# Experts in pairs, and half of the output columns combined on TensorE

## The reference

```python
scores = sigmoid(x2d @ router)               # (272, 64)
# keep 4 of 8 groups of experts, then the 8 best experts of each token
gate = take_along_axis(scores, idx); gate = gate / sum(gate) * 2.5
def expert_block(tok, e, gt):                # tok: the tokens that chose expert e
    y = (silu(x2d[tok] @ w_gate[e]) * (x2d[tok] @ w_up[e])) @ w_down[e]
    return y * gt[:, None]
routed = segment_sum(y, slot_tok)            # the 8 expert outputs of each token, added
f = swiglu(x2d, sh_gate, sh_up, sh_down) + routed
h = layer_norm(ALPHA * h + f, ln_ffn_g, ln_ffn_b)
```

## Time and profile before

| | |
|---|---|
| time, median of 3 runs | 1658.77 us (1658.12 to 1667.34) |
| span of the profiled execution | 1659.9 us |
| TensorE / weight loads / VectorE / ScalarE / GpSimd busy | 89% / 57% / 37% / 19% / 20% |
| mean granted TensorE clock | 0.968 |
| moved by DMA | 508.21 MB, mean 306 GB/s |
| expert loop, layer 0 / layer 1 | 388.5 to 902 us / 1102.5 to 1617 us |

### The profile page before, as it was taken

How to read it: one execution, slowest core, us unless ns; L and a number is a source line. 1 busy time by engine, 2 the same in 40 slices (tenths; PEclk the granted TensorE clock), 3 DMA queues, 4 the chain that set the end, 5 groups by cost and what they waited for, 6 DMA issues and landing times.

```text
span 1659.9 us, 33659 instructions
## 1 busy us (share of the span) xinstructions
PE 1469.7 (89%) x12824; PEld 952.7 (57%) x12824; DVE 619.0 (37%) x1580; ACT 318.7 (19%) x743; POOL 331.5 (20%) x412
## 2 busy tenths in 40 slices
PE   6989988899998888888888698999998888888886
PEld 4776877656665555555554267466655555555542
DVE  5362352673333333333332704543333333333327
ACT  1521332110111111111111015111111111111110
POOL 6012000021222222222221210122222222222210
PEclk9999988899999999999999799999999999999998
DMA  6330002349999999999997961299999999999986
GB/s 198 124 113 1 4 4 80 105 175 370 403 414 415 416 415 415 415 416 415 415 416 312 366 184 52 94 376 396 414 415 416 416 415 415 416 415 416 416 339 246
DMA packets 139862, 508.21 MB, mean 306 GB/s; under 512 B 29273, under 2 KB 58273, under 8 KB 104188
## 3 DMA queue, kind: packets, MB, share of 16 engines
q1 hardware_dynamic: 103312, 456.49, 68.9%
q0 software_dynamic: 22288, 41.89, 7.0%
q10 hardware_dynamic: 14172, 8.54, 1.8%
HBM read 501.38 MB, written 36.90 MB: 324 GB/s over the span
## 4 chain that ended last, share of the span: by engine, by line
PE 44%; SPq 23%; DMA 22%; DVE 6%; issue 3%; ACT 1%; ACTq 0%; DVEq 0%; POOL 0%; POOLq 0%
SPq L844 23%; DMA arena<-in_moe_w_up 21%; PE ps L781 9%; PE ps L1423 6%; PE ps L799 3%; PE ps L1553 3%; PE ps L1006 2%; PE ps L1865 2%; PE ps L1967 2%; PE ps L762 1%; PE ps L769 1%; PE ps L1748 1%; DMA arena<-routed 1%; PE ps L1849 1%; PE ps L998 1%
## 5 line engine op out<-in xcount | busy, mean ns | idle before, releaser
L781 PE MATMUL ps<-arena 128*64 128x256 f32 x2048 | 234.5, 381 | 57.2 <-DMA arena<-in_moe_w_up 57.2
L781 PE MATMUL ps<-ring,arena 128*64 128x256 f32 x2048 | 234.6, 381 | 51.8 <-DMA ring<-in_moe_w_up 38.5
L774 DVE COPY arena<-ps 128x512 f32<-128x512 f32 x128 | 88.6, 692 | 514.1 <-PE ps L769 514.1
L781 PEld LDWEIGHTS ps<-arena 128*64 128x64 f32 x2048 | 163.4, 137 | 151.5 <-issue 106.4
L818 POOL DMA_INDIRECT arena<-hrows,arena x128 | 129.7, 1013 | 586.0 <-DVE arena L814 572.0
L781 PEld LDWEIGHTS ps<-ring,arena 128*64 128x64 f32 x2048 | 154.5, 137 | 154.0 <-issue 79.0
L823 POOL DMA_INDIRECT routed<-arena x128 | 118.2, 924 | 240.2 <-DVE arena L942 175.8
L942 DVE TENSOR_SCALAR arena<-ps,arena 64x512 f32<-64x512 f32 x128 | 95.1, 743 | 162.1 <-PE ps L799 162.1
L896 ACT COPY arena<-ps 128x256 f32<-128x256 f32 x128 | 47.6, 372 | 537.0 <-PE ps L781 537.0
L906 ACT ACTIVATE arena<-ps,arena 64x512 f32<-64x512 f32 x128 | 87.5, 683 | 206.1 <-PE ps L799 206.1
L799 PE MATMUL ps<-ring,arena 128*64 128x512 f32 x512 | 124.0, 605 | 0.0
(11 more groups left out here) (375 smaller groups left out, 1595.4 us busy)
## 6 DMA issues: line engine op xcount, KB each, us to landing
ring<-in_moe_w_gate SPq DMA_DIRECT2D x64, 1024.0 KB
ring<-in_moe_w_up SPq DMA_DIRECT2D x64, 1024.0 KB
ring<-in_moe_w_down SPq DMA_DIRECT2D x64, 1024.0 KB
arena<-in_moe_w_gate SPq DMA_DIRECT2D x64, 1024.0 KB
arena<-in_moe_w_up SPq DMA_DIRECT2D x64, 1024.0 KB
arena<-in_moe_w_down SPq DMA_DIRECT2D x64, 1024.0 KB
arena<-routed SPq DMA_DIRECT2D x16, 1024.0 KB, 14.3
ring<-in_attn_w_qkv SPq DMA_DIRECT2D x6, 1024.0 KB
```

The source lines that it names most:

```text
L774: return nc.vector.tensor_copy(xgT.rearrange("p (r j) m -> p j r m", r=2), ps[:, bU, :].rearrange("p (j r m) -> p j r m", j=4, r=2))
L781: mm = nc.tensor.matmul(dst[SLOTS * j:SLOTS * j + SLOTS, 0:FF], xgT[:, k, :], slot_of(s + j)[:, FF * k:FF * k + FF], start=(k == 0), stop= ...
```

## The change

Experts are handled in pairs (the code says "duo"). A pair shares one set of marks, one pick (three matmuls with six columns of values in place of three), one gather of 128 whole rows and one scatter of 128 rows of 512 columns. The gathered rows are turned in two halves, in the turns of the two experts ahead, into one of two `xgT` buffers. Output columns 0 to 511 ("far") are scaled by the gate and scattered as before. Columns 512 to 1023 ("near") are only copied by ScalarE; VectorE builds a matrix `spread_T` of 128 slots by 272 tokens that holds the gates, and TensorE multiplies the two into the PSUM banks 1 and 7 (and bank 0 for the last 16 tokens), where all pairs add up over the loop. These matmuls (`pe_combine`) stand in the odd expert's turn, for the pair before. The second half of the shared expert is done whole in the turns of experts 0 and 1. After the loop, the shared expert's `down` is split likewise: three tiles with columns 0 to 511, and `mm_combine` for the rest (`sda`). The rows that are loaded back and added are 512 wide.

```diff
-HEAD = 5
-TAIL = 3
+HEAD = 4
+TAIL = 4
+DUOS = E // 2
+COLS = D // 2
...
-        routed = [nc.dram_tensor(f"routed{l}", (T * TOPK, D), F32, kind="Internal").ap() for l in range(2)]
-        hrows_d = [nc.dram_tensor(f"hrows{l}", (2 * T, D // 2), F32, kind="Internal").ap() for l in range(2)]
+        routed = [nc.dram_tensor(f"routed{l}", (T * TOPK, COLS), F32, kind="Internal").ap() for l in range(2)]
+        hrows_d = [nc.dram_tensor(f"hrows{l}", (T, D), F32, kind="Internal").ap() for l in range(2)]
...
-        bV, bU, bG, bR, bY = 0, 2, 3, 4, (5, 6)
+        bU, bG, bR, bY = 2, 3, 4, (5, 6)
+        bA = (1, 7)
+        few_acc = ps[:, 0, 0:P]
+        picked = ps[:, bG, FF:FF + 6]
...
+        def mm_turn_x(dst, rows, half):
             for j in range(4):
-                mm = nc.tensor.transpose(dst[:, P * j:P * j + P], rows[:, P * j:P * j + P], ident[:, :])
+                mm = nc.tensor.transpose(dst[:, P * j:P * j + P], rows[:, P * (4 * half + j):P * (4 * half + j) + P],
+                                         ident[:, :])
             return mm
-        def copy_xt():
-            return nc.vector.tensor_copy(xgT.rearrange("p (r j) m -> p j r m", r=2),
-                                         ps[:, bU, :].rearrange("p (j r m) -> p j r m", j=4, r=2))
+        def copy_xt(dst, half):
+            return nc.vector.tensor_copy(dst[:, 4 * half:4 * half + 4, :],
+                                         ps[:, bU, :].rearrange("p (c m) -> p c m", c=4))
...
+        def mm_combine(of_slots, rows, start, stop):
+            for t in range(NT - 1):
+                nc.tensor.matmul(ps[:, bA[t], :], of_slots[:, P * t:P * t + P], rows, start=start, stop=stop)
+            for q in range(4):
+                mm = nc.tensor.matmul(few_acc[32 * q:32 * q + META, :], of_slots[:, 2 * P:T], rows[:, P * q:P * q + P],
+                                      start=start, stop=stop, tile_position=(0, 32 * q))
+            return mm
...
+        def mark_slots(pos, first_slot):
+            for par in range(2):
+                cols = slice(SLOTS * par, SLOTS * par + SLOTS)
+                last = nc.vector.scalar_tensor_tensor(
+                    out=hot[:, :, cols], in0=iota_s[:, cols].unsqueeze(1).to_broadcast([P, NT, SLOTS]),
+                    scalar=float(first_slot + 1), in1=pos[:, :, par:par + 1].to_broadcast([P, NT, SLOTS]),
+                    op0=ALU.add, op1=ALU.is_equal)
+            return last
...
+        def take_index(at, gate_of):
+            for par in range(2):
+                rows = slice(SLOTS * par, SLOTS * par + SLOTS)
+                nc.vector.tensor_scalar(at[rows, :], picked[rows, 3 * par:3 * par + 2], OUT_OF_RANGE, None, ALU.add)
+                last = nc.vector.tensor_copy(gate_of[rows, :], picked[rows, 3 * par + 1:3 * par + 3])
+            return last
...
+        def spread_gates(gate_of):
+            return nc.vector.tensor_scalar(spread_T, iota_t, gate_of[:, 0:1], gate_of[:, 1:2], ALU.is_equal, ALU.mult)
...
+        def pe_pick(pe, L, a):
+            pe.wait_ge(L.onehot, duo_num(a, L.duo_base + 1))
+            wait(pe, L.index, duo_num(a, L.duo_base))
+            mm_pick(picked, values_of_duo(a)).then_inc(L.values, 1)
+        def pe_turn_x(pe, L, a, half):
+            b = a[1] // 2 % 2
+            if half == 0:
+                pe.wait_ge(L.gathered[b], duo_num(a, 8 * L.duo_base + 16, 16, 2))
+            wait(pe, L.xt_copied, num(a, 1, L.base + half))
+            mm_turn_x(ps[:, bU, :], xs[b], half).then_inc(L.xt, 1)
+        def pe_combine(pe, L, l, a):
+            pe.wait_ge(L.spread, duo_num(a, L.duo_base + 1))
+            pe.wait_ge(L.near, num(a, 1, L.base + 2))
+            if early(a, 0):
+                pe.wait_ge(*moe_dve[l].at("sm1"))
+            mm_combine(spread_T, near[a[1] // 2 % 2], early(a, 0), False).then_inc(L.combined, 1)
...
-            after, three_after, prev = ahead(e, 1), ahead(e, 3), e_before(e)
+            prev = e_before(e)
             if this:
                 s0, s1, _ = e_slots(e)
-                pe.wait_ge(L.xt_copied, num(e, 1, L.base + 1))
+                pe.wait_ge(L.xt_copied, num(first_of(e), 1, L.base + 2))
                 pe.wait_ge(slot_loaded[s0], num(e, 16, L.slot_base[s0] + 16, per=SETS))
                 pe.wait_ge(slot_loaded[s1], num(e, 16, L.slot_base[s1] + 16, per=SETS))
-                wait(pe, L.gu_copied, num(e, 1, L.base))
-                mm_gate_up(ps[:, bG, :], s0).then_inc(L.gu, 1)
-            if this and after:
-                pe_turn_x(pe, L, l, plus(e, 1))
-            if this and three_after:
-                pe_pick(pe, L, plus(e, 3))
-            if this:
+                if early(e, 0):
+                    pe.wait_ge(L.index, L.duo_base + 2)
+                else:
+                    wait(pe, L.gu_copied, num(e, 1, L.base))
+                if e[1] % 2 and exists(first_of(e, 2)):
+                    pe.wait_ge(L.index, duo_num(first_of(e, 2), L.duo_base + 1))
+                mm_gate_up(ps[:, bG, :], s0, xgT[e[1] // 2 % 2][:, :, side(e)]).then_inc(L.gu, 1)
+                if exists(first_of(e, 1)):
+                    pe_turn_x(pe, L, first_of(e, 1), e[1] % 2)
+                if e[1] % 2 and e_before(first_of(e)):
+                    pe_combine(pe, L, l, first_of(e, -1))
                 copied, hidden = num(e, 1, L.base + 1), num(e, 1, L.base)
                 if not isinstance(copied, int):
                     pe.reg_add(copied_count, copied_count, 1)
...
                     copied, hidden = copied_count, hidden_count
                 pe.wait_ge(*moe_dve[l].at("choice"))
                 pe.wait_ge(L.gu_copied, copied)
+                if e[1] % 2 == 0 and exists(first_of(e, 2)):
+                    pe_pick(pe, L, first_of(e, 2))
                 wait(pe, L.hid, hidden)
                 mm_turn(ps[:, bR, :]).then_inc(L.turned, 1)
...
-                act.wait_ge(L.index, num(q, 1, L.base + 1))
-                wait(act, L.scattered[q[1] % 4], num(q, 16, 4 * L.base, per=4))
-                nc.scalar.activation(ysc[q[1] % 4][:, 512:1024], ps[SLOTS:P, bY[q[1] % 2], :], ACT.Copy,
-                                     scale=gate_s[q[1] % 8][SLOTS:P]).then_inc(L.y_a, 1)
+                wait(act, L.combined, duo_num(first_of(q), L.duo_base - 1))
+                nc.scalar.copy(near[q[1] // 2 % 2][side(q), :], ps[other_side(q), bY[q[1] % 2], :]).then_inc(L.near, 1)
...
-                wait(dve, L.scattered[q[1] % 4], num(q, 16, 4 * L.base, per=4))
-                nc.vector.tensor_scalar(ysc[q[1] % 4][:, 0:512], ps[0:SLOTS, bY[q[1] % 2], :],
-                                        gate_s[q[1] % 8][0:SLOTS], None, ALU.mult).then_inc(L.y_v, 1)
+                dve.wait_ge(L.index, duo_num(first_of(q), L.duo_base + 1))
+                nc.vector.tensor_scalar(far[b][side(q), :], ps[side(q), bY[q[1] % 2], :], gate_s[b][side(q), 1:2], None,
+                                        ALU.mult).then_inc(L.far, 1)
...
             def turn(e):
-                if ahead(e, 3):
-                    pool_gather(pool, L, l, plus(e, 3))
+                if e[1] % 2:
+                    return
+                if exists(plus(e, 4)):
+                    pool_gather(pool, L, l, plus(e, 4))
                 if e_before(e):
-                    pool_scatter(pool, L, l, plus(e, -1))
+                    pool_scatter(pool, L, l, plus(e, -2))
             over_experts(pool, turn)
-            pool_scatter(pool, L, l, (0, E - 1))
+            pool_scatter(pool, L, l, (0, E - 2))
...
-                if early(e, 2):
+                    mm_shared(pe, l, "sg1", range(KC))
+                if early(e, 1):
                     pe.wait_ge(*moe_dve[l].at("sm0"))
-                if isinstance(e[0], int) and e[1] < 4:
-                    mm_shared(pe, l, ("sg1", "su1")[e[1] // 2], range(KC // 2 * (e[1] % 2), KC // 2 * (e[1] % 2) + KC // 2))
+                    mm_shared(pe, l, "su1", range(KC))
...
-                for u in range(6):
-                    r0, n = TILES[u // 2]
+                pe.wait_ge(main.index, main.duo_base + DUOS)
+                for u, (r0, n) in enumerate(TILES):
                     for j in range(2):
-                        m = mm_(ps[0:n, SD_BANKS[u], :], shm[:, j, r0:r0 + n],
-                                shared_w[2][:, D * j + 512 * (u % 2):][:, 0:512], start=(j == 0), stop=(j == 1))
+                        m = mm_(ps[0:n, SD_BANKS[u], :], shm[:, j, r0:r0 + n], shared_w[2][:, D * j:D * j + COLS],
+                                start=(j == 0), stop=(j == 1))
                     m.then_inc(*st.step("sd", u))
+                pe_combine(pe, main, l, (0, E - 2))
                 pe_spill(pe, l)
+                for j in range(2):
+                    m = mm_combine(shm[:, j, :], shared_w[2][:, D * j + COLS:D * j + D], False, j == 1)
+                m.then_inc(*st.step("sda"))
...
                     for k in ON_PE:
                         pe.wait_ge(routed_loaded[t][k // 2], 16 * (l + 1))
```

(19 more changed lines are left out.)

375 lines of the change are left out of this document (189 added, 186 removed).

## The result

The changed kernel takes 1679.61 us (median of 4 runs, 1672.39 to 1690.51) where the kernel before takes 1660.3 in the same rounds: a ratio of 1.011, 95% interval 1.007 to 1.015, so it is slower by some 1%. The forecast was 1640. The profiled execution is the fastest of the four: 1672.39 us with a span of 1670.7, against a span of 1659.9 before. So it shows 10.8 us of a loss whose median is 19.

The account below looks back on a forecast made before the run. The weight stream (DMA) was taken to bound the loop late on, TensorE close behind. Per layer -10.5 + 2.0 + 2.7 = -5.8 us, twice -11.6, and -7.5 behind the loops: -19, so 1640 us; range 1628 to 1664.

Parts of the forecast that it names:

- Behind the loop: From last gate/up to the end of the norms: 3 us less in one layer, 4.5 in layer 0; sum -7.5 us.
- say 0.5 for the spill test: Behind the loop, after the shared expert's combines: TensorE's overflow test was put at 0.5 us.
- The stream: DMA in the loop: halved scatter cuts q0 by a quarter, saving 10.5 us per layer; stream chain 497.4 us.
- TensorE in the loop: TensorE's cost in the expert loop: a pair goes from 13.86 to 15.3 us, 7.66 per expert; chain 487 us.
- the pick's wait for ScalarE's copy: In the loop, the pick waits for ScalarE's copy of the gate/up result, with the half-turn as cover: 0.1 us.
- The combine: New TensorE work once per pair in the loop: large matmuls 1.78 us, small ones 0.23, together 2.1 us.
- the first rival: TensorE bounds the loop (expert over 7.83 us); with weight loads exposed, combine 2.9 or 3.7 us: 1690 us; 11%.
- The first gate/up at half clock: Rival at each loop's start: first gate/up runs at half clock, 3.6 us more per layer, 1647 us; 20%.
- The start: Start of the loop: marks, index, larger gather and second half-turn delay the first gate/up by 2.7 us (1.4 to 3.5).
- The gather: Ahead of the first gate/up: first gather brings twice the bytes and takes 1.0 us more (0 to 1.5).
- The stream's idling in the first turns: Start of the loop: shared-expert work in turns 0 and 1 raises stream idling from 1.5 to 3.4 us, 2 more.
- a tile: Behind the loop: a token tile's norm and additions fall from 10.7 to 7.4 us as the additions halve.

Follow-up runs that it names:

- experiment 2: Changed kernel with the shared expert's combine issued ahead of TensorE's overflow test: 1678.84 us.
- 3: Changed kernel with the down matmuls of the expert before moved ahead of the pick in even turns: 1684.49 us.
- Experiment 4: Changed kernel with six fillers in place of four ahead of the first half-turn and one behind each half-turn: 1690.33 us.
- experiment 8: Changed kernel with the two large matmuls left out of the combine in all pairs but the first: 1672.41 us.
- (7): TensorE's unexecuted overflow pass cut to 33 matmuls (changed kernel, 1653.15 us), raised to 53 (kernel before, test moved ahead, 1672.29), cut to one wait (changed kernel, 1644.52).
- experiment 5: Kernel before with TensorE's overflow test moved ahead of the shared expert's 24 last matmuls: 1668.46 us.
- 6: Changed kernel with one more branch around the four overflow passes on every engine: 1654.62 us.
- the second of 9: Changed kernel with one branch around the four overflow passes and fillers at the first two half-turns, combines still behind the test: 1657.61 us, ratio 0.999.
- last version of experiment 9: Changed kernel with shared combines ahead of the test, fillers, and overflow passes as one loop under one branch (unrolled on VectorE): 1647.56 us, ratio 0.9935.
- experiment 1: Changed kernel with the overflow passes and their test left out on all engines: 1652.29 us; timed in rounds later, 1647.10 us, ratio 0.9947.

## Why the prediction was wrong

**The step that failed** is in "Behind the loop": "say 0.5 for the spill test". It measured 8.06 and 11.75 us of gaps in the profiled execution, 4.5 to 14.4 in others, and some 27 us for both layers in the median, with the lower clock behind the gaps. The number had no row: in the kernel before the test stood behind the shared expert's matmuls, and I neither bounded it from both sides nor looked for where its cost went. (The bounds that the prediction does give add up to 1630 to 1647 us, not 1628 to 1650; the result lies far outside either.) What lies behind the loops came out 11.0 and 15.7 us over the forecast, the loops 5.0 and 3.1. Cover is not the answer: 12 matmuls and a combine, 7.8 us, still stand ahead of the test where 24 matmuls in 10.7 us stood, and the old test without any of them cost 2.1 us. The new cost comes with the code: TensorE's overflow passes went from 29 to 61 matmuls and transposes because the change writes experts in pairs, on a path that isn't executed. I priced what the change adds to the loop and not what it adds to the code that is jumped over.

What is shown: the gaps at the test, by the code under its branches.

| matmuls and transposes in one pass on TensorE | gap, layers 0 / 1, us |
|---|---|
| 61, four branches, changed kernel | 8.06 / 11.75 |
| the same, experiment 2 (less VectorE's 2.5), 3, 4, 8 | 14.4 / 9.1, 7.88 / 12.88, 13.51 / 12.19, 9.91 / 4.5 |
| 53, four branches, kernel before (7) | 5.08 / 4.99 |
| 33, four branches, changed kernel (7) | 6.25 / 2.0 |
| 29, four branches, kernel before (5) | 2.09 / 2.22 |
| none, four branches, changed kernel (7) | 0 / 0 |
| 61, one branch around all (6, and the second of 9) | 1.16 + 2.67 / 0.88, 0.94 + 3.94 / 1.66 |

A single gap does not tell the length, since the 4.5 of the long code lies below the 6.25 of the short one. The sums of the two layers do: 14.4 to 25.7 us in five executions with 61, then 10.1, 8.3, 4.3 and 0. Each of the shorter versions has one profile only.

How the code comes to cost time is less clear. The page of the profile lists two queues of the kind "instruction" (q8, q14). Over the whole execution, the changed kernel and then the version with next to no code (7):

```profile
q8 instruction: 71, 1.16, 0.3%
...
q8 instruction: 64, 1.05, 0.3%
```

The two kernels differ in TensorE's passes alone, so seven packets of some 16 KB go with code that is never executed. All five profiles with the long passes have 71; in the kernel before it is 67, and 70 with the longer passes. That the wait for such packets is the gap is likely, and is not shown: the version with one loop (9) has two packets on q8 and one on q14 from 1613 to 1625 us, as many as the gap of 11.75 us, and waits there for VectorE alone (2.5 us). Open is also why the gaps differ so much between layers and executions.

The Trainium skill (Advanced Engine Details and Errata, Control Flow Timing) gives a compare-and-branch some 108 ns, 0.4 us for four. The run over hardly any code, where nothing shows, does not speak against it; the 8.06 and 11.75 us are far more. The Trainium skill (Advanced Engine Details and Errata, ISA Cache) gives cache lines of 16 KB, 256 instructions, of which there are two, but also 128 KB for TensorE. By the rows of a pair (6 + 8 + 64 + 4 + 16 + 12 matmul instructions, with a weight load each) a pass is some 220 instructions, nearly such a line, where one of an expert was some 104; an estimate from the Trainium skill's figure is 3.4 lines for four passes of a pair, 6.9 for both layers. No run here shows the lines.

**The stream** was right: q0 fell from 41.89 to 32.96 MB, and from 392 to 900 us from 17.16 to 12.72:

```profile
q0 software_dynamic: 6800, 12.72, 6.6%
```

Its packets fell too (9840 to 6800), which the prediction had not counted on. With TensorE out of the way (experiment 8) the loop took 497.7 us in the layer whose first gate/up ran at full clock, against 497.4.

**TensorE in the loop** was mis-sized by 0.5 us a pair: 15.82 in place of 15.3, nearly all of it in the pick's wait for ScalarE's copy (0.34) and the pick (0.10). The combine was right (2.15 for 2.1). At 7.91 us per expert the pair passes the 7.83 of the first rival, and TensorE does set the pace: in the last version of experiment 9 it holds 98% of the chain that ended last from 1110 to 1590 us. From the third gate/up (408.37) to the last (888.59) its 61 turns take 480.2 us, 7.87 each, since the last turns are shorter; with 9.1 and 10.3 us for the first two at full clock that is 499.5, where the prediction had 487. It is 2 us over the stream, and not the rival's 512 to 536. The rival's mechanism did not come true either: with loads in the open the combine would have taken 2.9 us or more (its 3.7 adds up to 3.6). The rule of the Trainium skill that spoke for it (TensorE: Matmul & The Clock Gate, Part 3 (The mechanism)) is not borne out by the combine's 2.15 us.

**The first gate/up at half clock**, given 20%, came true in both layers of the profiled execution, in part of its length: 6.51 and 5.08 us for 3.67. It is not so in every execution (3.67 us in both layers in experiment 1's timed version, which has no fillers). Experiment 4 gives 2.9 and 1.4 us back, where I had 3.6 each.

**The start** was right within a microsecond: +1.9 and +2.0 us of head, and from the first marks of layer 0 to the first gate/up +2.1, where 2.7 was forecast. The gather took less than thought (374.65 to 383.26 us, 0.35 more than before, for 1.0). The stream's idling in the first turns I get, at the prediction's 8.3 us per expert, as 1.2 us before and 2.8 after, for its 1.5 and 3.4; the 2.0 that it adds becomes 1.6.

**Behind the loop** but for the test: 46.7 to 47.5 us without it (experiment 1, both profiles), where 45 to 46 was forecast; a tile 7.98 us for 7.4.

With the test as cheap as it can be made, the last version of experiment 9 has a span of 1645.9 us, 14 below the kernel before. Of the 19 forecast it misses 3.7 in the loops (499.4 and 499.1 for 497.4) and 2.4 behind them (46.7 and 46.6 for 45.9 and 45).

## What to carry to other kernels

On TensorE here, a branch over code that never runs had a price that grew with the length of that code and with the number of branches: put one test around all of a rare path and write it as a loop. When a change moves or halves the work behind which a step hides, price that step as if it stood in the open, by an experiment if no row shows it. Here that alone would have given 2.1 us a layer (experiment 5), so look as well at what the change does to the code that is skipped. And where two bounds end within 2% of each other, count every small wait in both: half a microsecond per pair made TensorE's chain 12.5 us longer than forecast and decided which engine set the pace.

## What was not expected of the hardware

TensorE's time over skipped code: 4.5 to 14.4 us a layer for four jumps over the long passes, 0.9 to 1.7 us for one jump over all of them, with 2.7 to 3.9 more behind it in layer 0, and none that shows over next to no code. The gap also takes the clock down: the granted clock from 1624 to 1636 us was 0.65, and the combine behind it took 3.78 us in place of 1.98.

```profile
1624.00:1636.00 12.00, 0.25 (x9) 0.12 (x1) 0.00 (x0) 0.00 (x0) 0.00 (x0) 0.65 0.82 321
```
